# A transformer block kernel with product-key experts: gates by adding indirect DMAs instead of one-hot matmuls

## What is computed

```python
sub = jnp.einsum("thpc,hpnc->thpn", qh, peer_sub_keys)          # 8 heads, 2 x 128 keys
v1, i1 = lax.top_k(sub[:, :, 0], 16);  v2, i2 = lax.top_k(sub[:, :, 1], 16)
cand = (v1[..., :, None] + v2[..., None, :]).reshape(T, 8, 256)
vals, cidx = lax.top_k(cand, 16)
experts = e1 * 128 + e2                                         # of 16384
gates = jax.nn.softmax(vals, axis=-1)
h = jnp.einsum("cd,chkd->chk", xc, u_sel)
a = jax.nn.gelu(h, approximate=False) * gc
y = jnp.einsum("chk,chkd->cd", a, v_sel)
```

## Time and profile before

| | |
|---|---|
| time of the runs, median of 3 | 3205.39 us (3203.41 to 3206.05) |
| span of the profiled execution (no other time of it is given) | 3203.0 us |
| PE busy | 3185.0 us, 17362 matmuls |
| DVE busy | 2226.0 us |
| ACT busy | 1555.5 us |
| POOL busy | 13.7 us, 29 instructions |
| moved by DMA | 610.61 MB, mean 191 GB/s |

### The profile page before, as it was taken

The page is one execution under the profiler, slowest core; times in us unless marked ns, Lnnn a source line. Parts: engine busy times, 40 slices in busy tenths (PEclk is TensorE's granted clock), DMA queues, the critical chain, the costliest instruction groups (busy, mean ns, idle before and its releaser), DMA issues.

```text
span 3203.0 us, 42378 instructions
## 1 busy us (share of the span) xinstructions
PE 3185.0 (99%) x17362; PEld 2707.6 (85%) x17362; DVE 2226.0 (69%) x3055; ACT 1555.5 (49%) x1998; POOL 13.7 (0%) x29
## 2 busy tenths in 40 slices
PE   9999999999999999999999999999999999999999
PEld 8888888888888888887888888888888788888887
DVE  6775556677577567766568997766687787865564
ACT  4564444555355455546544555455443344444353
POOL 0000000000000000000000000000000000000000
PEclk9999999999999999999999999999999999999999
DMA  7456665656665666653555666666666665556665
GB/s 252 154 162 218 211 211 180 210 191 191 191 190 190 193 188 192 205 170 111 190 154 171 217 216 189 188 183 224 190 190 212 203 200 173 188 184 192 194 184 171
DMA packets 175825, 610.61 MB, mean 191 GB/s; under 512 B 19201, under 2 KB 27553, under 8 KB 174736
## 3 DMA queue, kind: packets, MB, share of 16 engines
q1 hardware_dynamic: 173648, 599.93, 60.0%
q0 software_dynamic: 1984, 7.99, 0.8%
HBM read 597.36 MB, written 10.49 MB: 190 GB/s over the span
## 4 chain that ended last, share of the span: by engine, by line
PE 97%; DVE 2%; ACT 1%; issue 0%; DMA 0%; SPq 0%; ACTq 0%; DVEq 0%
PE PS L1194 29%; PE PS L1211 16%; PE PS L1213 16%; PE PS L1212 16%; PE PS L1191 15%; PE PS L1414 1%; PE PS L1427 1%; PE PS L1293 1%; DVE LO L1749 0%; PE PS L1247 0%; PE PS L1326 0%; ACT UN L1506 0%; ACT HI L1436 0%; PE PS L1305 0%; PE PS L1223 0%
## 5 line engine op out<-in xcount | busy, mean ns | idle before, releaser
L1749 DVE TENSOR_TENSOR LO<-RAW,HI 128x1024 fp32r<-128x1024 f32 (+1 forms) x1096 | 1325.1, 1218 | 698.0 <-ACT HI L1436 694.7
L1436 ACT ACTIVATE HI<-RAW 128x1024 fp32r<-128x1024 f32 (+1 forms) x1096 | 1148.3, 1054 | 1044.6 <-PE PS L1213 732.5
L1194 PE MATMUL PS<-XX,HI 128*128 128x512 f32 x4032 | 968.4, 391 | 0.0
L1194 PEld LDWEIGHTS PS<-XX,HI 128*128 128x128 f32 x4032 | 739.4, 188 | 145.1 <-issue 2.4
L1211 PE MATMUL PS<-HI,FH 128*128 128x512 f32 x1760 | 692.0, 393 | 1.7 <-DVE LO L1749 1.7
L1213 PE MATMUL PS<-HI,FL 128*128 128x512 f32 x1760 | 685.8, 390 | 0.0
L1212 PE MATMUL PS<-LO,FH 128*128 128x512 f32 x1760 | 684.7, 389 | 0.0
L1191 PEld LDWEIGHTS PS<-XX,LO 128*128 128x128 f32 x4032 | 520.2, 191 | 21.1 <-issue 1.0
L1191 PE MATMUL PS<-XX,LO 128*128 128x256 f32 x4032 | 536.8, 284 | 0.0
L1213 PEld LDWEIGHTS PS<-HI,FL 128*128 128x128 f32 x1760 | 330.3, 188 | 70.1
L1211 PEld LDWEIGHTS PS<-HI,FH 128*128 128x128 f32 x1760 | 330.3, 188 | 69.1 <-DVE LO L1749 2.2
(11 more groups left out here) (286 smaller groups left out, 1667.7 us busy)
## 6 DMA issues: line engine op xcount, KB each, us to landing
RAW<-in_peer_ut SPq DMA_DIRECT2D x256, 512.0 KB, 4.1
RAW<-in_peer_v SPq DMA_DIRECT2D x256, 512.0 KB, 4.2
RAW<-in_ffn_w_up SPq DMA_DIRECT2D x176, 512.0 KB, 4.2
RAW<-in_w_in SPq DMA_DIRECT2D x88, 512.0 KB, 4.3
RAW<-in_ffn_w_down SPq DMA_DIRECT2D x88, 512.0 KB, 4.2
RAW<-in_w_in_c SPq DMA_DIRECT2D x48, 512.0 KB, 3.7
RAW<-in_w_mix_out SPq DMA_DIRECT2D x32, 512.0 KB, 4.0
RAW<-in_w_in_2c SPq DMA_DIRECT2D x32, 512.0 KB, 3.7
```

Source lines behind the costliest of these rows:

```text
L1194: m = e.matmul(o, hi[:, k, x], XX[:, 4 * u + k, :, :].rearrange("p h s -> p (h s)"), start=first and k == 0, stop=last and k == 3, skip_gr ...
L1436: return e.activation(dst, src, ACT.Copy) if scale is None else e.activation(dst, src, ACT.Copy, scale=scale)
L1749: return e.tensor_tensor(dst, src, hi.bitcast(F32), ALU.subtract)
```

## The change

- The gates are no longer made by PE. A DRAM tensor of 16384 x 256 elements (expert, token) is filled with zeros, by 32 DMAs of 512 KB from DRAM to DRAM, one after each of the first 32 products of the first feed-forward layer (`zero`, SP).
- `choose` gets a last step `address`: DVE computes (128 x second + first) x 256 + token for 32 choices of each of 128 tokens. Then POOL issues 32 indirect DMAs (`scatter`), each of 128 single elements, one to a partition, which are added to what stands in DRAM. Before the first of each head it waits for the landing of all earlier ones of the same half of the tokens. There are 256 such DMAs. The rate of the selection falls from 0.68 to 0.45 a unit.
- All eight up chunks come first, in the order 3, 4, 5, 6, 7, 0, 1, 2; the activations of 3 to 7 are stored in DRAM (20 stores in place of 8). Then come all eight down chunks.
- POOL loads the gates of chunks 1 and 0 (`gates_in`, 8 x 512 KB) once everything has been added. SP loads the gates of chunks 2 to 7 (`gates_later`, 24 x 512 KB) and the activations of 3 to 7 (`back`, 20 x 512 KB) between weights. DVE multiplies the two in place (`later_mul`), and `split_up` does the rest for all chunks but 1.
- The constants lose 112 columns of key numbers and gain two with the token numbers. `up` and `down` weights are streamed in the new order of the chunks; their number and form stay.
- `tables`, `onehot`, `gates_sum`, `gates_out`, `gates_side`, `gates_aside`, `gates_back`, `x`, `gelu`, `weigh` and `split_aside` are gone.

In the list, in units: the eight `scatter` steps stand after units 580, 600, 620, 640, 660, 680, 700 and 720, and `gates_in` after 720. The first `first_mul` stands after unit 816, the first `second_mul` after 818 (before: 724 and 726). The zeros stand after units 203 to 359. `gates_later` of chunk 2 stands after 839; for chunk 3, loads after 874 to 877, `later_mul` after 882 to 885, `split_up` after 930 to 936, and the same again every 32 units up to chunk 7.

The diff, cut to its core:

```diff
+NKEY = 128
+ZEROS = 32
+UP_ORDER = (3, 4, 5, 6, 7, 0, 1, 2)
+DOWN_ORDER = (1, 0, 2, 3, 4, 5, 6, 7)
...
-    order = [("up", c) for c in (3, 4, 0, 1, 2)] + [("down", c) for c in (1, 0, 2, 3, 4)]
-    order += [(d, c) for c in range(5, 8) for d in ("up", "down")]
+    order = [("up", c) for c in UP_ORDER] + [("down", c) for c in DOWN_ORDER]
...
+    zeroed = [0]
     for n, th in enumerate(THIRDS):
         for q in th:
             for i in range(2):
                 for b in range(2):
                     product(("f", q, i, b), 4)
+                    if zeroed[0] < ZEROS:
+                        emit("zero", zeroed[0])
+                        zeroed[0] += 1
...
+        emit("address", t, g)
+        emit("scatter", t, g)
...
-    rate[0] = 0.68
+    rate[0] = 0.45
...
-    def first_pass():
-
-        emit("onehot", 0, 0)
-        yield
-        for blk in range(32):
-            if blk < 31:
-                emit("onehot", 0, blk + 1)
-            yield
-            me = ("gates_sum", blk)
-            spare(me, 0, (ACT_, ("gates_out", blk), 3))
-            emit(*me)
-            emit("gates_out", blk)
-            if blk:
-                emit("gates_aside", blk - 1)
-        emit("gates_aside", 31)
...
-        rate[0] = 0.5
-        yield from first_pass()
...
+    def first_gates():
+        for c in (1, 0):
+            for j in range(4):
+                emit("gates_in", c, j)
+        yield
+
     background.extend([first_gates(), first_blocks()])
-    for c in (3, 4, 0, 1, 2):
+    for c in UP_ORDER:
         up_staged(c)
     flush()
...
     rate[0] = 1
-    background.extend([gates_back(2), multiply_third()])
-    down(1, then=0)
-    background.append(gates(2, 3))
-    down(0, then=2)
-    beside.append(gates_back(3))
-    down(2, then=3)
-    down(3, then=4)
-    background.extend([pause(4), gates(3, 3)])
-    down(4)
-    for c in range(5, 8):
+    def multiply(c):
+        yield from pause(2)
         for j in range(4):
-            for i in range(2):
-                product(("x", c, j, i), 4)
-            evacuations.append(hidden(c, j))
-        down(c)
+            emit("gates_later", c, j)
+            emit("back", c, j)
+            yield
+        yield from pause(4)
+        for j in range(4):
+            emit("later_mul", c, j)
+            yield
+
+    for j in range(4):
+        emit("gates_later", 2, j)
+    background.append(multiply_third())
+    for i, c in enumerate(DOWN_ORDER):
+        if 1 <= i < 6:
+            background.append(multiply(DOWN_ORDER[i + 2]))
+        down(c, DOWN_ORDER[i + 1] if i < 7 else None)
...
+    UPS = {3: UF, 4: STAGE, 5: UF, 6: STAGE, 7: UF, 0: GM[2], 1: STAGE, 2: UF}
+    UNDER = {5: 3, 6: 4, 7: 5, 1: 6, 2: 7}
+    HELD = {0: 2, 2: 0, 3: 2, 4: 0, 5: 2, 6: 0, 7: 2}
+    ASIDE = (3, 4, 5, 6, 7)
...
+            elif kind == "zero":
+                n, = k
+                e.dma_start(GATES[:, 1024 * n:1024 * n + 1024], a["zeros"]).then_inc(l_zero, 16)
+            elif kind == "gates_later":
+                c, j = k
+                for t in range(2):
+                    w.wait_ge(l_scatter[t], 256 * 8)
+                w.wait_ge(s_dve, {2: V("second_mul", 3), 3: V("third_mul", 3)}[c] if c < 4 else V("later_mul", c - 1, 3))
+                e.dma_start(GM[1][:, 4 * j:4 * j + 4, :].rearrange("p c s -> p (c s)"),
+                            GATES[:, 4096 * c + 1024 * j:4096 * c + 1024 * j + 1024]).then_inc(l_gates[2][j], 16)
             elif kind == "back":
                 c, j = k
                 w.wait_ge(l_aside[c, j], 16)
-                w.wait_ge(s_mm, multiplied(("y", c - 1, 3), 2 * j + 1))
-                e.dma_start(blocks(UF, j).rearrange("p k s -> p (k s)"), a["aside"][c - 3, j]).then_inc(l_back[j], 16)
+                w.wait_ge(s_dve, V("split_up", c - 2 if c > 4 else {3: 0, 4: 2}[c], 3))
+                e.dma_start(blocks(GM[HELD[c]], j).rearrange("p k s -> p (k s)"), a["aside"][c - 3, j]).then_inc(
+                    l_back[HELD[c], j], 16)
             elif kind == "store":
                 c = slice(512 * k[0], 512 * k[0] + 512)
...
+            elif kind == "scatter":
+                t, g = k
+                w.wait_ge(l_zero, 16 * ZEROS)
+                w.wait_ge(s_dve, V("address", t, g))
+                for h in (2 * g, 2 * g + 1):
+                    if h:
+                        w.wait_ge(l_scatter[t], 256 * h)
+                    for i in range(16 * h, 16 * h + 16):
+                        e.indirect_dma_start(a["gates"], bass.IndirectOffsetOnAxis(IDX[:, t, i:i + 1], 0),
+                                             TK[:, t, i:i + 1], None, compute_op=ALU.add).then_inc(l_scatter[t], 16)
+            elif kind == "gates_in":
+                c, j = k
+                for t in range(2):
+                    w.wait_ge(l_scatter[t], 256 * 8)
+                e.dma_start(GM[1 if c else 0][:, 4 * j:4 * j + 4, :].rearrange("p c s -> p (c s)"),
+                            GATES[:, 4096 * c + 1024 * j:4096 * c + 1024 * j + 1024]).then_inc(l_gates[1 if c else 0][j], 16)
...
-            elif kind == "gates_sum":
-                blk, = k
-                i = blk % 2
-                w.wait_ge(s_dve, V("onehot", 0, blk))
-                for s, n in until_free(step):
-                    w.wait_ge(s, n)
-                for j in range(8):
-                    o = spare(step)[:, 64 * j:64 * j + 64]
-                    for part in range(3):
-                        m = e.matmul(o, OH2[:, i, j // 2, :, j % 2], GOH1[:, i, j // 2, part, :, j % 2],
-                                     start=part == 0, stop=part == 2, skip_group_check=True)
-                m.then_inc(s_pe, 1)
...
+            elif kind == "address":
+                t, g = k
+                first, second = (TK[:, t, 128 * n + 32 * g:128 * n + 32 * g + 32] for n in (1, 2))
+                w.wait_ge(l_const, 16)
+                w.wait_ge(s_dve, V("gate", t, g))
+                e.scalar_tensor_tensor(out=first, in0=second, scalar=float(NKEY), in1=first, op0=ALU.mult,
+                                       op1=ALU.add).then_inc(s_dve, 1)
+                w.wait_ge(s_dve, V("address", t, g, k=1))
+                e.tensor_scalar(IDX[:, t, 32 * g:32 * g + 32], first, float(S), const("token")[:, t:t + 1], ALU.mult,
+                                ALU.add).then_inc(s_dve, 1)
             elif kind == "first_mul":
                 j, = k
                 w.wait_ge(s_act, A("us_gelu", 0, j))
-                w.wait_ge(s_act, A("gates_out", 31))
+                w.wait_ge(*gates_landed(0, j))
...
             elif kind == "split_up":
                 c, j = k
-                w.wait_ge(s_mm, multiplied(("y", 1 if c == 0 else 0, 3), 2 * j + 1))
-                w.wait_ge(s_dve, V("first_mul", j) if c == 0 else V("third_mul", j))
-                copy(blocks(FH, j), blocks(GM[2] if c == 0 else GM[0], j)).then_inc(s_act, 1)
-            elif kind == "split_aside":
-                c, j = k
-                w.wait_ge(s_mm, multiplied(("y", c - 1, 3), 2 * j + 1))
-                w.wait_ge(s_dve, V(*step, k=1))
-                copy(blocks(FH, j), HB[:]).then_inc(s_act, 1)
-            elif kind == "gelu":
-                c, j = k
-                for i in range(2):
-                    w.wait_ge(s_dve, V("x", c, j, i))
-                    d = HB[:, 2 * i:2 * i + 2, :]
-                    e.activation(d, d, ACT.Gelu).then_inc(s_act, 1)
-            elif kind == "weigh":
-                c, j = k
-                w.wait_ge(s_mm, multiplied(("y", c - 1, 3), 2 * j + 1))
-                w.wait_ge(s_dve, V("weigh", c, j, k=1))
-                copy(blocks(FH, j), HB[:]).then_inc(s_act, 1)
+                w.wait_ge(s_mm, multiplied(("y", down_before(c), 3), 2 * j + 1))
+                w.wait_ge(s_dve, V("later_mul", c, j) if c > 2 else V("first_mul", j) if c == 0 else V("third_mul", j))
```

More of the change, by code:

```diff
@@ L128 @@
     "best": (0, 0, 5), "cand0": (0, 0, 8), "cand1": (0, 0, 6), "pick0": (0, 0, 7), "pick1": (0, 1, 6),
[L129 to L132, removed]
+    "gate": (0, 0, 3), "address": (0, 0, 2),
+    "us": (0, 1, 1), "us_gelu": (0, 1, 0), "first_mul": (0, 1, 1), "second_mul": (0, 1, 2), "third_mul": (0, 0, 1), "later_mul": (0, 0, 1), "split_up": (0, 1, 1),
+    "y": (0, 0, 2),
 }
@@ L652, in plan @@
         background.extend(choose(t, g) for t in range(2))
[L654 to L696 removed]
+    staged = [[] for _ in range(8)]
     def first_blocks():
@@ L725, in multiply_third @@
     def multiply_third():
-        yield from pause(3)
+        yield from pause(6)
         for j in range(4):
@@ L740, in from_chip @@
             yield from pause(2)
-    def from_aside(c):
-        yield from pause(2)
-        for n in range(5):
-            if n < 4:
-                emit("back", c, n)
-            if n:
-                emit("split_aside", c, n - 1)
-            yield from pause(2)
     def down(c, then=None):
@@ L753, in down @@
             if g == 3 and then is not None:
```

(19 more changed lines are left out.)

206 lines of the change are left out of this document (30 added, 176 removed).

## The result

| | before | changed |
|---|---|---|
| median of 4 runs | 3205.72 us (3203.41 to 3206.46) | 3146.24 us (3144.86 to 3147.88) |
| span of the profiled execution | 3203.0 us | 3143.9 us |

What follows compares the result with a forecast made beforehand. TensorE's queue was taken to bound the kernel: span 3203.0 - 26.7 - 32.0 = 3144.3 us, plus 2.4 us for the median of the runs, 3146.7, forecast 3147 us, all else hidden; range 3141 to 3197.

Steps and rivals of the forecast that it cites:

- TensorE's queue, 26.7 + 32.0 us: One-hot matmuls and transposes leave TensorE: 26.7 us beside first-pass up products, 32.0 us in the second and third pass.
- VectorE's relief: VectorE loses the one-hot tables and block evacuations; it bounds nothing, so this was worth nothing by itself.
- The runs 2.4 us above the span: The median of the runs was taken to lie 2.4 us above the profiled span, giving 3146.7 us.
- Issue of an indirect DMA, 1.2 us against a limit of 2.34: GpSimd's 256 adding DMAs: 1.2 us an issue, hidden up to 2.34 us before chunk 0's gates are needed.
- The heads' landings, 14 of 3.6 us: GpSimd waits 14 times for a head's DMAs to land, 3.6 us each, before the gates are loaded.
- Element packets, between nothing and 0.177 us, a third taken (0.059): DMA engine time per scattered element: up to 363 us per engine at the bound; a third taken, costing nothing.
- the rival of crowding: Scattered elements crowd the DMA engines and weights come late: TensorE waits 20 to 50 us, 3167 to 3197; chance 0.11.
- Zeros, 1.3 to 2.8 us a copy, hidden: 32 DRAM to DRAM copies of 512 KB in the first feed-forward stage, room 5.9 us each: cost nothing.
- SyncE's burst, nothing: Gates, activations and weights loaded within four units leave SyncE's queue 4.8 us behind; weights land in 9.0: nothing.
- VectorE and GpSimd holding each other up: During selection, 256 holds of 0.5 us on the shared port stall VectorE 35 us, time 3182; chance 0.09.
- a sign of being wrong: Low halves on VectorE taking over 1.22 us between 1720 and 2170 us would show the prediction wrong.
- the first rival: Late gates stop VectorE at the first gate products; each 0.1 us above 2.34 per issue costs 25.6 us; chance 0.14.

Runs made afterwards that it cites:

- Runs 1 and 2: The kernel before with one matmul left in each block: of 24 in the first pass, 3182.57 us; of 8 in the second and third, 3185.76 us.
- the run at 0.28: The changed kernel with the selection at 0.28 steps a unit in place of 0.45, so the last indirect DMAs go later: 3216.54 us, ratio 1.0036 to the kernel before.
- Run 3: The changed kernel with its 256 indirect DMAs writing in place of adding: 3145.7 us, ratio 0.9814 to the kernel before.
- run 4: The changed kernel with three more 512 KB DRAM to DRAM copies behind each of the 32 zero copies: 3148.66 us, ratio 0.983 to the kernel before.
- run 8: The changed kernel with a chunk's eight loads of gates and activations in a row in SyncE's queue, ahead of the weights: 3146.65 us.
- run 9: The changed kernel with a chunk's eight loads in a row and two 512 KB DRAM to DRAM copies behind each activation load: 3193.6 us.
- Runs 10 and 11: The changed kernel with one more VectorE instruction behind each low half of units 724 to 789: both inputs in SBUF, 3144.32 us; one in PSUM, 3148.5 us.

## Why the prediction was right, and which terms were off

- *TensorE's queue, 26.7 + 32.0 us.* Right. Span 3203.0 - 58.7 = 3144.3 forecast, 3143.9 measured. Runs 1 and 2 show that the two excesses were the blocks', all but 1.7 us: the 0.50 for each of the 64 side blocks was 0.47 of place in the queue, and the rest the two waits for low halves, which left too. So VectorE's relief, put at nothing, was worth 1.7 us; the sum is whole because it was taken from the length of the stretch. The pitch was the right price: the durations of the earlier trace rows add up to 62.1 us, near the sum but by chance, 33.3 for the side blocks that took 30.3 and 28.8 for the others that took 26.0.
- *The runs 2.4 us above the span.* 1.8 for the profiled execution of the changed kernel (3145.72 against 3143.9); the median came out 0.8 us under the forecast.
- *Issue of an indirect DMA, 1.2 us against a limit of 2.34.* Mis-sized, the largest miss. It is 1.54 alone, 1.85 with the waits for VectorE, and 0.30 follows each: 2.15 from one to the next. The limit left room for 0.19, not for 1.1. So the last group was through at 2298 instead of 2150, and GpSimd was busy for 492 us instead of some 300. The choice, twice the plain DMA of the earlier trace rows, was an estimate without a row, and I gave the case where it fails 0.14. That it cost nothing is in part luck: the pitch was nearly twice my price, and 60 us were left. With this pitch at hand the chance would have been higher, and the plan's rate looked at more closely: the run at 0.28 shows that a last issue 155 us later decides the sign.
- *The heads' landings, 14 of 3.6 us.* 8 waits, 25.4 us together, and 2.8 before the loads. Of the 14, six are for the first head of a group, and the head before it on that half of the tokens was issued a whole group earlier; only the second heads wait, eight of them.
- *Element packets, between nothing and 0.177 us, a third taken (0.059).* 0.050 us by the window at rate 0.28. Run 3 gives the same from the other side: 3.0% of 3144 us less on each engine for 28672/16 = 1792 packets less, 0.053. The elements took about 100 us of each engine and stood beside the weights. TensorE waits for no weight and no low half beside them, so the rival of crowding is out. The Trainium skill, "DMA: Bandwidth & Descriptors", section "Bandwidth", gives about 10.5 ns a packet, worked out for a load of 4 KB in 64 packets, and I took it for a floor of any transfer. By an estimate from it the elements would have held the engines for 344 us; the trace does not agree, 50 ns on one engine is 3 ns over sixteen.
- *Zeros, 1.3 to 2.8 us a copy, hidden.* Hidden, and 0.75 to 1.1 us (run 4).
- *SyncE's burst, nothing.* Right, by both reserves (run 8); loads landed in 7.0 to 8.0 us, under the 9.0 expected. Room for eight more transfers there was not (run 9).
- *VectorE and GpSimd holding each other up.* Half right, but the half that costs nothing. GpSimd waits, up to 1.07 us an issue (2615 ns against 1541). VectorE does not, but for 0.07 us five times: the 1.29 us at most are over the 1.22 that I had named as a sign of being wrong, and nothing came of it. So no stall of VectorE could come from it; what it did was to eat 80 us (256 times 0.31) of the slack of the first rival. The Trainium skill, "SBUF — State Buffer", section "SBUF: two separate sides", says that whichever comes first holds the shared port pair for its whole instruction, and that two SBUF inputs count if GpSimd reads SBUF. Runs 10 and 11 agree for GpSimd waiting, to the hundredth of a microsecond. For VectorE waiting through a whole GpSimd instruction, the traces disagree: low halves that start during an issue of 1.54 us take their usual 1.23 at most.

## What to carry to other kernels

When an engine is busy 99% of the span, work taken out of its queue is worth its pitch, not its duration, and also the break that it makes in a row of large matmuls. What the work is moved to must be priced with the same care although it lies off the path: find the place where its result is first used, work out the latest start, and divide. Here the limit of 2.34 us an issue against a true 2.15 was the whole question, and one constant of the plan (0.45 or 0.28) decided between 1.8% faster and 0.4% slower.

## What was not expected of the hardware

- An indirect DMA of 128 single elements keeps GpSimd for 1.54 us when it adds and 0.95 when it writes, with 0.30 between two. Adding sends one packet per element, writing one per eight.
- Its issue waits for a running VectorE instruction with two SBUF inputs. In the changed kernel: low halves at 2128.20 and 2130.97, each 1.23 long; issues at 2128.35 and 2131.14 of 2.49 and 2.46 us; issues that start clear of one, 1.54. The duration is the rest of the low half plus 1.41. The writing form of run 3 keeps the same rule with 0.83.
- One small bfloat16 matmul in a row of large ones costs TensorE 0.11 us (up products) or 0.15 us (down products), of which 0.03 to 0.04 are its own and the rest the break.
- A copy of 512 KB from DRAM to DRAM took 1.1 us of the DMA engines in run 4 and about 0.75 in the changed kernel, less than the 1.31 us of a 512 KB load at the best rate of before.
- After a stop of 63.5 us TensorE's first eight matmuls ran at a granted clock of 0.50 and took 3.78 us in place of 2.00.
